# Values of the second attention as three fp32r products, asked for ten chunks behind the scores

## The reference, cut to what matters

```python
h = _modulate(_rmsnorm(xs, norm_g[l]), shift, scale)       # 256 x 2048
p = h @ w_l                                                  # q, k, v, z_a, u_b, z_b, g_a, g_b
q = _rope(_rmsnorm(q, q_norm_g), cos, sin) * q_scale
k, v = concat(k of x, k of ctx), concat(v of x, v of ctx)    # 512 keys
s = einsum('bqhgd,bkhd->bhgqk', q, k)
w = softmax(s)
o = einsum('bhgqk,bkhd->bqhgd', w, v)                        # 12 heads x 256 x 128
y_a = (o * silu(z_a)) @ w_pa
y_b = (fourier_mix(u_b) * silu(z_b)) @ w_pb
y = (sigmoid(g_a) * y_a + sigmoid(g_b) * y_b) @ w_o
```

## Time and profile before

| | us |
|---|---|
| median of 3 runs | 2181.99 |
| lowest and highest run | 2180.74, 2184.23 |
| the profiled execution, its own time | 2181.22 |
| span of that execution in the profile | 2179.4 |
| PE busy | 2169.7 (100%) |
| PEld busy | 2039.5 (94%) |
| DVE busy | 1559.3 (72%) |
| ACT busy | 1067.9 (49%) |
| POOL busy | 122.1 (6%) |

### The profile page before, as it was taken

One profiled execution on the slowest core, in us unless ns is written; L12 is line 12 of the kernel. 1 busy time (PEld: TensorE's weight loads), 2 busy tenths in 40 slices (PEclk: granted clock), 3 DMA queues, 4 the chain that ended last, 5 costly groups with the idle time before them and its releaser, 6 DMA issues.

```text
span 2179.4 us, 37464 instructions
## 1 busy us (share of the span) xinstructions
PE 2169.7 (100%) x15829; PEld 2039.5 (94%) x15829; DVE 1559.3 (72%) x1916; ACT 1067.9 (49%) x1413; POOL 122.1 (6%) x111
## 2 busy tenths in 40 slices
PE   9999999999999999999999999999999999999998
PEld 9999999999999889989988988998889999999987
DVE  6889788888989587544554555555768787776776
ACT  5554345544444566544443543444655555444443
POOL 1000000000000400000000000000101111110101
PEclk9999999999999999999999999999999999999999
DMA  8766877687787956565656666656755545678784
GB/s 268 231 215 214 253 256 231 223 279 257 255 286 260 235 180 194 184 203 184 203 193 194 185 203 202 195 188 208 248 168 167 164 140 174 220 257 303 255 278 156
DMA packets 245247, 474.43 MB, mean 218 GB/s; under 512 B 17718, under 2 KB 22704, under 8 KB 244568
## 3 DMA queue, kind: packets, MB, share of 16 engines
q1 hardware_dynamic: 239720, 453.85, 64.8%
q0 software_dynamic: 5280, 18.17, 2.9%
q10 hardware_dynamic: 80, 0.03, 0.0%
HBM read 467.77 MB, written 5.78 MB: 217 GB/s over the span
## 4 chain that ended last, share of the span: by engine, by line
PE 96%; DMA 1%; DVE 1%; ACT 0%; issue 0%; SPq 0%; DVEq 0%; POOLq 0%; POOL 0%; ACTq 0%
PE ps L1008 20%; PE ps L1010 20%; PE ps L1009 20%; PE ps L1001 11%; PE ps L1003 10%; PE ps L1002 10%; PE ps L901 1%; DMA raw<-in_w_out 1%; DMA vsu<-in_b_ada 0%; PE ps L824 0%; PE ps L761 0%; PE ps L811 0%; PE ps L890 0%; PE ps L889 0%; PE ps L891 0%
## 5 line engine op out<-in xcount | busy, mean ns | idle before, releaser
L1008 PE MATMUL ps<-op0h,whiW 128*128 128x256 f32 x3200 | 887.3, 277 | 0.1
L1010 PE MATMUL ps<-op0h,wloW 128*128 128x256 f32 x3200 | 883.6, 276 | 0.0
L1009 PE MATMUL ps<-op0l,whiW 128*128 128x256 f32 x3200 | 883.5, 276 | 0.0
L1441 DVE TENSOR_TENSOR wloW<-raw,whiW 128x1024 fp32r<-128x1024 f32 (+1 forms) x501 | 615.5, 1241 | 293.4 <-ACT whiW L1069 290.9
L1069 ACT ACTIVATE whiW<-raw 128x1024 fp32r<-128x1024 f32 (+1 forms) x501 | 524.4, 1055 | 579.6 <-PE ps L1010 455.9
L1008 PEld LDWEIGHTS ps<-op0h,whiW 128*128 128x128 f32 x3200 | 600.7, 188 | 1.9 <-issue 0.7
L1009 PEld LDWEIGHTS ps<-op0l,whiW 128*128 128x128 f32 x3200 | 600.7, 188 | 0.6
L1010 PEld LDWEIGHTS ps<-op0h,wloW 128*128 128x128 f32 x3200 | 600.7, 188 | 0.0
L1441 DVE TENSOR_TENSOR wloT<-raw,whiT 128x1024 fp32r<-128x1024 f32 (+1 forms) x264 | 320.2, 1221 | 233.9 <-ACT whiT L1069 232.7
L1069 ACT ACTIVATE whiT<-raw 128x1024 fp32r<-128x1024 f32 (+1 forms) x264 | 275.0, 1050 | 283.2 <-PE ps L1003 224.8
L1001 PE MATMUL ps<-whiT,op1h 128*128 128x512 f32 (+1 forms) x672 | 259.3, 386 | 0.2 <-DVE wloT L1441 0.2
(11 more groups left out here) (345 smaller groups left out, 2122.7 us busy)
## 6 DMA issues: line engine op xcount, KB each, us to landing
raw<-in_w_in SPq DMA_DIRECT2D x253, 512.0 KB, 4.4
raw<-in_w_up SPq DMA_DIRECT2D x128, 512.0 KB, 4.1
raw<-in_w_down SPq DMA_DIRECT2D x128, 512.0 KB, 3.9
raw<-in_w_ada SPq DMA_DIRECT2D x96, 512.0 KB, 4.7
raw<-in_w_gate SPq DMA_DIRECT2D x96, 512.0 KB, 4.9
raw<-in_w_out SPq DMA_DIRECT2D x64, 512.0 KB, 5.5
raw<-in_w_branch SPq DMA_DIRECT2D x48, 512.0 KB, 4.9
raw<-in_w_proj_a SPq DMA_DIRECT2D x24, 512.0 KB, 5.1
```

Of the source, the lines that this page charges most:

```text
L1008: pe.matmul(o, wh, xh[:, ka, :], start=first and m % 2 == 0, stop=False, skip_group_check=True)
L1009: pe.matmul(o, wh, xl[:, ka, :], start=False, stop=False, skip_group_check=True)
L1010: mm = pe.matmul(o, wl, xh[:, ka, :], start=False, stop=last, skip_group_check=True)
L1441: v.tensor_tensor(wlo[job.mode][q % NSPL][:, :, 0:job.n], x, h.bitcast(F32), ALU.subtract).then_inc(s_lo, 1)
```

## The change

The values of the second attention are no longer plain float32 products. The exps are split into a high part (`prob_high`, a copy to float32r on ACT) and a low part (`prob_low`, a subtraction on DVE, in place of the exps), v of tokens and context likewise (`split_v`), and PE makes three float32r products for each tile of keys, 12 a head. The order of a pair's parts changes: maxima from step q + 1 to q + 2, high parts at q + 6, low parts at q + 7, values on PE from q + 7 to q + 10, share from q + 8 to q + 10, the product out of bank 4 from q + 9 to the front of q + 11, the split of the result from q + 10 to q + 12. `totals2` on POOL waits for the low parts (`s_pl`) and no longer for the sums. Pairs 1, 2, 3 and 5 (`CLOSE`) exchange the banks of even and odd head, do the context's keys first, and wait for `s_atv` in the middle of the odd head's scores. The rope tables are kept once and not four times, one of four rot buffers goes, ga and gb stand in other places, some semaphores are merged, and epilogues of zb, za2, ga0/ga1 and gb1 get waits for values already taken.

```diff
+CLOSE = (1, 2, 3, 5)
...
+        for name, q in (("vc", of["k"].end + 3), ("vx", of["vx"].end + 2)):
+            for tt in range(2):
+                side(act_at, q + tt, "split_v", name, tt)
+                side(dve_at, q + 1 + tt, "split_v", name, tt)
...
-                side(dve_at, q + 1, "softmax2_max", h)
+                side(dve_at, q + 2, "softmax2_max", h)
                 side(dve_at, q + 4, "softmax2_less", h)
                 side(act_at, q + 5, "softmax2_exp", h)
-                side(pe_at, q + 7, "values2", h)
                 side(dve_at, q + 6, "softmax2_sum", h)
-            side(dve_at, q + 8, "softmax2_share", i)
+                side(act_at, q + 6, "prob_high", h)
+                side(dve_at, q + 7, "prob_low", h)
+            side(dve_at, q + 10, "softmax2_share", i)
+            dve_at[q + 11][0:0] = [("values2", (2 * i,)), ("values2", (2 * i + 1,))]
             for h in (2 * i, 2 * i + 1):
-                side(dve_at, q + 9, "values2", h)
-                side(act_at, q + 10, "values2", h)
-                side(dve_at, q + 10, "values2_low", h)
+                side(pe_at, q + 10, "values2", h)
+                side(act_at, q + 12, "values2", h)
+                side(dve_at, q + 12, "values2_low", h)
...
             def totals2(i):
-                pool.wait_ge(s_sum2, 2 * i + 2)
+                pool.wait_ge(s_pl, 2 * i + 2)
...
+                close = h // 2 in CLOSE
                 if h >= 2:
-                    pe.wait_ge(s_scr2, h - 1)
-                    if e == 0:
+                    pe.wait_ge(s_scr2, h - e)
+                    if e == 0 and not close:
                         pe.wait_ge(s_atv, h)
...
-                for st in range(4):
+                for st in (2, 3, 0, 1):
+                    if st == 0 and e == 1 and close:
+                        pe.wait_ge(s_atv, h - 1)
...
             def values2(h):
-                pe.wait_ge(s_exp2, h + 1)
+                pe.wait_ge(s_pl, h + 1)
+                o, ph, pl = bank[4][:, 256 * e:256 * e + 256], probh[e][h // 2], probl[e]
                 for st in range(4):
-                    mm = pe.matmul(bank[4][:, 256 * e:256 * e + 256], vv[:, st % 2, 128 * kv:128 * kv + 128], keyed[e][:, st, :],
-                                   start=st == 0, stop=st == 3)
+                    pe.matmul(o, vh, ph[:, st, :], start=st == 0, stop=False)
+                    pe.matmul(o, vh, pl[:, st, :], start=False, stop=False)
+                    mm = pe.matmul(o, vl, ph[:, st, :], start=False, stop=st == 3)
...
+            def prob_high(h):
+                act.wait_ge(s_exp2, h + 1)
+                act.activation(probh[e][i][:, :, :], keyed[e][:, :, :], ACT.Copy).then_inc(s_ph, 1)
...
+            def prob_low(h):
+                v.wait_ge(s_ph, h + 1)
+                v.wait_ge(s_sum2, h + 1)
+                v.tensor_tensor(probl[e][:, :, :], p[:, :, :], probh[e][h // 2][:, :, :].bitcast(F32), ALU.subtract).then_inc(s_pl, 1)
...
             def values2(h):
-                v.wait_ge(s_av2, h + 1)
+                v.wait_ge(s_av2, h - e + 2)
                 v.tensor_tensor(x, bank[4][:, 256 * e:256 * e + 256], total[:, e, :], ALU.mult).then_inc(s_atv, 1)
```

More of the change, by code:

```diff
@@ L410, in program @@
         vx = bg("vx", [128, 2, 512], 40)
-        rct = bg("rct", [128, 2, 512], 44)
-        rst = bg("rst", [128, 2, 512], 48)
+        rct = bg("rct", [128, 2, 128], 44)
+        rst = bg("rst", [128, 2, 128], 45)
+        vxh, vxl, vcl = bg("vxh", [128, 2, 512], 46, F32R), bg("vxl", [128, 2, 512], 40, F32R), bg("vcl", [128, 2, 512], 4, F32R)
+        vch = [bg("vch0", [128, 512], 50, F32R), bg("vch1", [128, 512], 67, F32R)]
+        probh = [[bg(f"probh{r}", [128, 4, 256], 8 + r, F32R) for r in rows] for rows in ((8, 8, 8, 8, 4, 4), (12, 12, 0, 0, 0, 0))]
+        probl = [at(f"probl{e}", [128, 4, 256], tmp_at + 4096 * e, F32R) for e in range(2)]
         ub = bg("ub", [128, 2, 512], 52)
@@ L417, in program @@
         peak, total = at("peak", [128, 2, 256], tmp_at + 10240), bg("total", [128, 2, 256], 69)
-        rot = [bg(f"rot{i}", [128, 512], 61 + 2 * i) for i in range(4)]
+        rot = [bg(f"rot{i}", [128, 512], 61 + 2 * i) for i in range(3)]
         mgh, mgl = bg("mgh", [128, 16, 256], 24, F32R), bg("mgl", [128, 16, 256], 40, F32R)
-        ga = [bg(f"ga{i}", [128, 4, 256], 56 + 4 * i) for i in range(2)]
-        gb = [bg(f"gb{i}", [128, 4, 256], 64 + 4 * i) for i in range(2)]
+        ga = [bg(f"ga{i}", [128, 4, 256], 56 + 8 * i) for i in range(2)]
+        gb = [bg(f"gb{i}", [128, 4, 256], 60 + 8 * i) for i in range(2)]
         gbc = bg("gbc", [128, 2048], 0)
@@ L454, in turned_x0, with scores_bank @@
             return bank[4 + (u + 1) % 3][:, 256 * j:256 * j + 256]
+        def scores_bank(h, j):
+            e = h % 2 if h // 2 not in CLOSE else 1 - h % 2
+            return bank[4 + 2 * e + j]
         def half(ps):
@@ L502, in program @@
         s_sig = sem("z_sigmoid")
-        s_sc2, s_scr2, s_max2, s_peak2, s_less2, s_exp2, s_sum2, s_total2, s_share2, s_av2, s_atv, s_ahi, s_att = (
-            sem("scores2"), sem("scores2_read"), sem("max2"), sem("max2_all"), sem("scores2_less"), sem("exp2"), sem("sum2"), sem("sum2_all"),
+        s_ph, s_pl, s_vh, s_vl = sem("prob_high"), sem("prob_low"), sem("values_high"), sem("values_low")
+        s_sc2, s_scr2, s_max2, s_pool2, s_less2, s_exp2, s_sum2, s_share2, s_av2, s_atv, s_ahi, s_att = (
+            sem("scores2"), sem("scores2_read"), sem("max2"), sem("peaks_and_totals2"), sem("scores2_less"), sem("exp2"), sem("sum2"),
             sem("share2"), sem("values2"), sem("att_gated"), sem("att_high"), sem("att_operand"))
@@ L1193, in scores2 @@
                 for i in range(2):
-                    op = act.activation(keyed[e][:, 2 * i:2 * i + 2, :], half(bank[4 + 2 * e + i]), ACT.Copy)
+                    op = act.activation(keyed[e][:, 2 * i:2 * i + 2, :], half(scores_bank(h, i)), ACT.Copy)
                 op.then_inc(s_scr2, 1)
@@ L1200, in softmax2_exp, with split_v @@
                 act.activation(p[:, :, :], p[:, :, :], ACT.Exp, scale=ATT_SCALE).then_inc(s_exp2, 1)
+            def prob_high(h):
+                e, i = h % 2, h // 2
+                act.wait_ge(s_exp2, h + 1)
+                if i == 4:
+                    act.wait_ge(s_share2, 4)
+                elif i == 2:
+                    act.wait_ge(s_share2, 2)
+                if h >= 2:
+                    act.wait_ge(s_av2, h - 1)
+                act.activation(probh[e][i][:, :, :], keyed[e][:, :, :], ACT.Copy).then_inc(s_ph, 1)
+            def split_v(name, tt):
+                x, h = ((vc[:, tt, :], vch[tt][:, :]), (vx[:, tt, :], vxh[:, tt, :]))[name == "vx"]
+                if name == "vc":
+                    act.wait_ge(s_pair[of["vc"].pair], of["vc"].after)
+                else:
+                    act.wait_ge(s_pair[of["vx"].pair], of["vx"].after)
+                act.activation(h, x, ACT.Copy).then_inc(s_vh, 1)
             def values2(h):
@@ L1220, in _ @@
                      "turn1": turn1, "values1": values1, "scale_qk": scale_qk, "turn_qk": turn_qk, "scores2": scores2, "softmax2_exp": softmax2_exp,
-                     "values2": values2, "fourier_t": fourier_t, "fourier_d": fourier_d, "split_kc": split_kc}
+                     "values2": values2, "prob_high": prob_high, "split_v": split_v, "fourier_t": fourier_t, "fourier_d": fourier_d, "split_kc": split_kc}
             def ep_copy(job, b0, b1):
@@ L1345, in ep_silu @@
                     act.wait_ge(s_xw, 16)
+                elif job.arg == 8:
+                    act.wait_ge(s_av2, 7)
+                elif job.arg == 12:
+                    act.wait_ge(s_av2, 4)
                 for i, b in ((0, b0), (1, b1)):
@@ L1358, in ep_gate2 @@
                     act.wait_ge(s_qkt, 10)
-                    if which == "b" and c == 1:
+                    if c == 1:
+                        act.wait_ge(s_av2, 12)
                         act.wait_ge(s_atv, 12)
@@ L1608, in top_rounds @@
                 if r == 0:
-                    v.wait_ge(s_cm, 16)
+                    v.wait_ge(s_cm, 48)
                     v.wait_ge(s_idxs, 12)
@@ L1748, in rotate @@
             def rotate(s, tt):
-                t1, t2 = rot[tt], rot[2 + tt]
-                sv, dv, rv = (x.rearrange("p (a h f) -> p a h f", h=2, f=32) for x in (t1[:, :], t2[:, :], rst[:, tt, :]))
+                t1, t2 = rot[tt], rot[2]
+                sv, dv = (x[:, :].rearrange("p (n a h f) -> p n a h f", a=2, h=2, f=32) for x in (t1, t2))
+                rv = rst[:, tt, :].rearrange("p (a h f) -> p a h f", h=2, f=32).unsqueeze(1).broadcast_to([128, 4, 2, 2, 32])
                 if s == 1 and tt == 0:
```

60 lines of the change are left out of this document (33 added, 27 removed).

## The result

The changed kernel takes 2199.11 us (median of 3 runs, 2199.09 to 2199.89) against 2181.99 before: ratio 1.0082, interval 1.0068 to 1.0095. It is slower, by 17.1 us; the prediction said 2188 (2178.5 to 2192). The profiled execution took 2199.89 us, 18.7 over that of before.

The account below looks back on a forecast made before the run. TensorE was taken to bound the kernel, other engines mattering only when it waits. Terms: -3.5 - 0.3 + 2.1 + 3.5 + 0.5 + 2.9 + 1.35 = +6.5 us on 2181.99, forecast 2188 us, range 2178.5 to 2192.

Parts of the forecast that it names:

- values, six pairs: PE's 24 value products take 2.87 us a pair instead of 3.46, saving 0.59 us x 6 = 3.5 us.
- stall of pair 1: PE waits in the odd head's scores for DVE's product of pair 0's values: 2.1 us, floor 1.2.
- stall of pair 2: The same wait for pair 1's values, with DVE starting late: 3.5 us, 0.7 without carried delay and hold.
- stall of pair 3: The same wait for pair 2's values: 0.5 us, floor nothing.
- pairs 4 to 5: The same wait in pair 5: products end at 7.6 against the mark of 7.76 us, so nothing.
- Fourier stretch, head 8: DVE runs late with pair 3's share: lows 0.7 and 0.3, fourier_d(3) 0.4, head 8's wait 1.5; 2.9 us, floor 0.
- behind pair 5: PE waits for low halves delayed by the later share: 1.35 us, in place of a gap of 0.27.
- (a): Rival: stalls shrink to their floors and cancel the gain, 2181.2 to 2186 us; chance 0.40.
- (b): Rival: DVE keeps up, no stall decides and the gain comes whole, 2176.5 to 2178.5 us; chance 0.09.
- (c): Rival: late DVE delays ACT's score copies and highs, one to three more waits, 2191 to 2197 us; chance 0.09.
- lows 22 and 26: Chunk low halves on DVE with 0.9 and 0.65 us left; if these go, more waits of 1 to 3 us.

Follow-up runs that it names:

- early-sum kernel: The changed kernel with GpSimd's sums over partitions waiting for VectorE's sums again and no longer for the low parts: 2187.28 us, ratio 1.0036.
- root-first kernel: The changed kernel with GpSimd's two roots of qq2 placed between the maximum and the sum of pair 3: 2197.08 us, ratio 1.0073.
- again: The changed kernel run once more with no edit, in another set: 2200.17 us, ratio 1.0087.
- waits filled: The changed kernel with TensorE repeating 12 score products in head 3 and 24 in head 5 ahead of the wait: 2197.52 us, ratio 1.0076.

## Why the prediction was wrong

The direction was right and the size was not: +6.5 us forecast, +17.1 measured. The terms, against what PE's timeline of the profiled execution shows (a gap counts less its normal distance of 0.11 or 0.12). This adds up PE's own time, and not what each term costs by itself:

```
term                      forecast   measured
values, six pairs         -3.5       -3.5
stall of pair 1            2.1        2.15
stall of pair 2            3.5        3.9
stall of pair 3            0.5        0.8
pairs 4 to 5               0          0
Fourier stretch, head 8    2.9        3.45 + 0.8 + 0.4 + 1.75 = 6.4
behind pair 5              1.1        1.15
low clock                  -          1.7 + 1.4 + 2.9 = 6.0
early chunk, by chance     -          1.2
sum                        6.5        18.1 of 18.7
```

**TensorE's own part: right.** The values' 24 products run 0.12 us apart. PE's timeline from the first of them to the chunk behind (pair 0), 2.87 us as forecast from the earlier trace rows:

```profile
1670.06 0.28 PE L922 MATMUL ps<-probh,vxh 128*128 128x256 f32 x1
1670.18 0.28 PE L923 MATMUL ps<-probl,vxh 128*128 128x256 f32 x1
...
1672.82 0.28 PE L924 MATMUL ps<-probh,vcl 128*128 128x256 f32 x1
1672.93 0.28 PE L1030 MATMUL ps<-op0h,whiW 128*128 128x256 f32 x1
```

**The stalls of pairs 1 to 3: right in place and releaser, and near in size, but pair 2's size by luck.** VectorE's timeline follows the order I wrote out: a low half held beside the sum, the epilogue, the reciprocal, the products at 1679.18 for a forecast 1678.3.

```profile
1667.14 5.54 DVE L1486 TENSOR_TENSOR wloW<-raw,whiW 128x1024 fp32r<-128x1024 f32 x3
...
1673.94 3.34 DVE L1845 RECIPROCAL total<-total 128x512 f32<-128x512 f32 x1
...
1679.18 0.75 DVE L1875 TENSOR_TENSOR keyed<-ps,total 128x256 f32<-128x256 f32 x2
1681.80 0.42 DVE L1801 TENSOR_TENSOR rot<-rot,rst 128x256 f32<-128x256 f32 x1 [1.88 <-ACT rot L1195]
```

But I charged pair 2's delay to VectorE's backlog, with rotations straight behind the products at 1679.0. They began at 1681.80, 1.88 us idle on ScalarE, which waited 7.11 for the root. With an early sum, and so an early root, that stall is 0.7 us for 3.9, so the forecast 3.5 came near for a reason that does not carry it.

**The step that failed: the Fourier stretch, "2.9, floor 0".** I made the sum of pair 3 late and followed who waits for it: VectorE's share. I did not follow who stands behind it in GpSimd's own queue. That was the root of qq2, not held by any semaphore of the change, but by order and by the changeover of 7.9 us. From there the chain runs ScalarE's scaling (11.06 us idle), its copy for the Fourier product, PE. PE's gaps there come to 6.4 us for the forecast 2.9, and its products run slower besides. The early-sum kernel shows this by its edit of one wait, and the root-first kernel shows that the changeover is the price and not the sum's place alone. By PE's starts the early sum's 11.8 us are 3.2 up to the end of pair 2's wait, 1.3 behind it up to pair 3's, 6.3 from there to head 8 (61.28 us for 67.55) and 1.1 behind pair 5. The Trainium skill, "GPSIMD Engine Reference", section 2.1 (Instruction dispatch), says that the first call of a freshly loaded GpSimd kernel pays a code load of about 6 us that no profile row shows. The traces here have 6.8 to 8.7 us of "issue" from the end of a reduction to the TENSOR_TENSOR behind it, and not at the first alone; that this idle time is such a load no run here shows.

**The second omission: the clock.** I priced each stall at its length. Behind gaps of 2.27, 4.02 and 3.57 us between starts the granted clock fell to the 1.2 GHz level, and PE's work took 6.0 us longer in this trace, 4.0 in the second one of the same kernel. What of that reaches the time is another question. The us from the end of one wait of PE to the end of the next, from its timelines:

```
                                   changed kernel   again    waits filled
pair 1's wait to pair 2's          42.49            42.35    42.58
  slower by the low clock          1.7              0        0
pair 2's wait to pair 3's          38.21            39.06    36.94
  slower by the low clock          1.4              2.4      0
Fourier stretch's wait to head 8   23.31            23.32    23.30
  slower by the low clock          2.9              1.6      1.7
```

Behind pair 1 the 1.7 us cost 0.1 us or less, because PE comes to its waits that much later and waits that much less. Behind pair 2 nearly all of it is paid: 1.3 and 2.1 us. Before head 8, 2.9 and 1.6 us give the same distance, so at least that difference is not paid; no trace has this gap and the full clock behind it, so whether the rest is stays open. What the low clock cost in time is thus shown for 1.3 us of this trace and 2.1 us of the second.

**The rivals.** (a), stalls and gain cancel, and (b), VectorE keeps up, are refuted by the waits. (c), the delay feeds on itself, came nearest in size, but not by its mechanism: about the lows 22 and 26 that it named stands one gap of 0.72 us in one of two traces, none in the other.

**What is left open.** 0.6 us of the 18.7 are not assigned. Why the root begins 6.8 us after one sum and 8.1 after another was not tried. What decides whether the clock falls behind a gap between 2.27 and 3.76 us was not tried either.

## What to carry to other kernels

When a change delays an instruction, list what stands behind it in its own engine's queue, not only who waits on its semaphore; on GpSimd, add the idle "issue" time between two kinds of instruction, which a trace may hide in one place and show in another. A stall of TensorE of over 2 us can have the low clock behind it, which made PE's work 1.4 to 3.0 us longer each time here; it costs time only where no later wait takes it back, 1.3 us behind one stall and nothing behind another in the same trace. A saving on the bounding engine is worth nothing ahead of a wait that another engine sets: here the same three products were worth 0, 1.8 and 3.1 us as the waits were taken out.

## What the runs showed of the hardware

- GpSimd stands idle 6.8 to 8.7 us from the end of a PARTITION_ALL_REDUCE to the start of the next TENSOR_TENSOR (7.95 and 7.92 in the changed kernel), and 7.45 us the other way (root ahead of the sum), with no row for it.
- In the second attention of these traces TensorE's clock fell to 1.2 GHz, for 2.8 to 6.0 us of its work, behind every gap of 3.9 us and more between starts, never behind one of 2.14 us or less, and behind some between: three of four of 2.27 us, not the one of 2.99 us, six of seven of 3.56 to 3.76 us. The Trainium skill, "TensorE: Matmul & The Clock Gate", Part 1, gives the activity gate these two levels and nothing between; the traces agree, as the windows' 0.6 are parts of a stretch at either: 0.50 in one that lies whole in the low clock (1721.90 to 1726.70).
- Three products of 256 columns on rounded operands take 0.36 us where one fp32 product takes two records and 0.43 us.
